# The gated mixer of the second block: 64-column cells instead of 128-column tiles, two step programs instead of one

## The reference

```python
def gated_delta_rule(q, k, v, g, beta):            # mixer A, 4 heads, chunks of 64
    decay = where(causal, exp(gcum_i - gcum_j), 0)
    lmat = where(strict, einsum(kb, kc) * decay, 0)
    uw = triangular_solve(lmat + eye, concat([vb, kb * exp(gcum)], -1))
    attn_intra = einsum(qc, kc) * decay
    def step(state, xs):
        v_new = u_ - w_ @ state
        o = qd @ state + a_ @ v_new
        state = state * exp(gl) + kd.T @ v_new

def mlstm_chunkwise(q, k, v, i_log, f_log):        # mixer B, 4 heads, chunks of 64
    def step(carry, xs):
        pmat = qk_ * exp(d_ - mt)
        num = inter * (q_ @ c_st) + pmat @ v_
        den = inter * (q_ @ n_st) + sum(pmat, -1)
        hout = num / maximum(abs(den), exp(-mt))
        c_st = sc * c_st + kw.T @ v_
        n_st = sc * n_st + sum(kw, -2)

def mixer_ab(hn, ...):
    proj = hn @ w_in                               # 1024 -> 4112
    qkv = silu(causal_conv(proj_a, conv_w)); qa, ka = l2norm(q), l2norm(k)
    oa = rmsnorm(gated_delta_rule(...), norm_a) * silu(z)
    ob = rmsnorm(mlstm_chunkwise(...), norm_b) * sigmoid(o_gate)
    return concat([oa, ob], -1) @ w_out
```

## Time and profile before

| | us |
|---|---|
| median of 3 runs | 3643.74 (3643.6 to 3644.13) |
| the profiled execution | 3643.23 |
| its span (first to last instruction) | 3641.0 |
| TensorE busy / VectorE / ScalarE / GpSimd | 3367.5 / 1598.1 / 1181.9 / 132.3 |
| mean granted TensorE clock | 0.938 |
| projection of the mixer, first L420 to the output projection's first | 1874.4 to 2373.8 |

### The profile page before, as it was taken

The page is one execution under the profiler, slowest core; times in us unless marked ns, Lnnn a source line. Parts: engine busy times, 40 slices in busy tenths (PEclk is TensorE's granted clock), DMA queues, the critical chain, the costliest instruction groups (busy, mean ns, idle before and its releaser), DMA issues. The chain is left out here.

```text
span 3641.0 us, 41271 instructions
## 1 busy us (share of the span) xinstructions
PE 3367.5 (92%) x16842; PEld 2672.2 (73%) x16842; DVE 1598.1 (44%) x2420; ACT 1181.9 (32%) x1910; POOL 132.3 (4%) x148
## 2 busy tenths in 40 slices
PE   7888899999998899999978999989999877899998
PEld 5555577888887566788867787878887655688886
DVE  2144544334354355545553533144334436444344
ACT  2134433223133244433343423133223424432232
POOL 0012200000000021000000210000000000000000
PEclk9899999999998999999977999579999887889999
DMA  6500014432222100223221111013222120122321
GB/s 249 199 1 1 7 56 146 145 122 82 64 70 75 58 1 30 86 93 99 93 68 42 47 35 47 1 64 95 97 93 87 52 73 1 64 70 94 98 94 63
DMA packets 73354, 269.43 MB, mean 74 GB/s; under 512 B 8136, under 2 KB 9032, under 8 KB 71888
## 3 DMA queue, kind: packets, MB, share of 16 engines
q1 hardware_dynamic: 73168, 266.80, 21.8%
HBM read 264.67 MB, written 2.10 MB: 73 GB/s over the span
## 5 line engine op out<-in xcount | busy, mean ns | idle before, releaser
L420 PE MATMUL PS<-room,WHI 128*128 128x512 f32 (+1 forms) x7200 | 2050.1, 382 | 53.5 <-DVE room L704 13.8
L420 PEld LDWEIGHTS PS<-room,WHI 128*128 128x128 f32 x7200 | 1273.1, 192 | 345.8 <-issue 96.4
L420 PE MATMUL PS<-room,WLO 128*128 128x512 f32 (+1 forms) x3600 | 1246.8, 376 | 0.0
L420 PEld LDWEIGHTS PS<-room,WLO 128*128 128x128 f32 x3600 | 641.3, 191 | 127.1
L376 DVE TENSOR_TENSOR WLO<-RING,WHI 128x1024 fp32r<-128x1024 f32 x371 | 453.8, 1223 | 375.5 <-ACT WHI L367 374.6
L367 ACT ACTIVATE WHI<-RING 128x1024 fp32r<-128x1024 f32 x371 | 389.9, 1053 | 544.6 <-PE PS L420 530.7
L826 DVE SCALAR_TENSOR_TENSOR H<-PS,VEC,H 128x511 f32<-128x511 f32 (+1 forms) x132 | 83.1, 657 | 310.1 <-ACT H L804 310.1
L804 ACT ACTIVATE H<-PS,VEC 128x512 f32<-128x512 f32 (+1 forms) x132 | 88.4, 704 | 351.2 <-PE PS L420 351.2
L1257 PE MATMUL PS<-room 96*128 96x256 f32 (+1 forms) x432 | 154.3, 476 | 11.2 <-ACT SQ L1368 7.7
L763 DVE SCALAR_TENSOR_TENSOR X<-PS,MOD,X 128x512 f32<-128x512 f32 x96 | 60.5, 658 | 219.9 <-PE PS L420 219.8
L1463 DVE TENSOR_REDUCE room<-PS 128x1 f32<-128x768 f32 (+1 forms) x120 | 101.9, 849 | 99.1 <-PE PS L1257 98.6
(11 more groups left out here) (344 smaller groups left out, 2988.3 us busy)
## 6 DMA issues: line engine op xcount, KB each, us to landing
RING<-in_stream SPq DMA_DIRECT2D x370, 512.0 KB, 3.4
room<-in_w_ada SPq DMA_DIRECT2D x84, 512.0 KB, 5.6
H<-in_w_ada SPq DMA_DIRECT2D x12, 512.0 KB, 4.5
room<-in_consts SPq DMA_DIRECT2D x4, 1024.0 KB, 9.7
room<-in_wq SPq DMA_DIRECT2D x2, 1728.0 KB, 7.5
X<-in_x_in SPq DMA_DIRECT2D x2, 1536.0 KB, 10.2
room<-in_wple SPq DMA_DIRECT2D x2, 1024.0 KB, 4.8
out_dram<-H SPq DMA_DIRECT2D x8, 256.0 KB, 2.0
```

What stands on the lines that cost most here:

```text
L420: mm = pe.matmul(acc, wt[:, w], xt[:, k * xw + lo:k * xw + lo + q], start=(k == 0 and z == 0), stop=(k == kt - 1 and z == 2))
```

## The change

The chunk matrices of mixer A and B (`LT`, `ATT`, `T`, `TT`, `Y`, `BT`, `DEC`, `DECB`, `ATB`) are no longer 128 wide block diagonals. Chunk n lies as a 64x64 cell on partitions 0 to 63 (n even) or 64 to 127 (n odd), four cells side by side, so that a head's matrix is 256 columns wide and not 512. VectorE, ScalarE and GpSimd work on 256 columns there. On TensorE each matmul of 128x128 becomes two of 64x64, whose rows and output partitions are those of the chunk: even chunks use the first quarter of the array, odd ones the last.

The generators are two for each engine (`pe_chain` and `pe_side`, and so on), both advanced at each tick; a step waits for its tick with `until`. The side program has the query norms, the key by query matrices, the value transposes and A's final spread. `product(i)` and `update(i-1)` now share a tick. Mixer A's first chunk starts the state with a copy and the last makes no state; in B the same, B's state alternates between two buffers, the denominators gather in bank 6 and are taken once at the end. The order of units puts B's values first and A's gate z last.

```diff
-AB_UNITS = ([("gates", 0)] + [("A", 4 + h) for h in range(4)] + [("A", h) for h in range(4)] + [("A", 8 + h) for h in range(4)]
-            + [("A", 12 + h) for h in range(4)] + [("B", h) for h in range(8)] + [("B", 12 + h) for h in range(4)]
-            + [("B", 8 + h) for h in range(4)])
+AB_UNITS = ([("gates", 0)] + [("B", 12 + h) for h in range(4)] + [("A", 4 + h) for h in range(4)] + [("A", h) for h in range(4)]
+            + [("A", 8 + h) for h in range(4)] + [("B", h) for h in range(8)] + [("B", 8 + h) for h in range(4)]
+            + [("A", 12 + h) for h in range(4)])
...
+    cell = lambda name, h, n: c.a(o[name] + h * HALF + (n // 2) * CHUNK, CHUNK, *rows(n))
+    rows = lambda n: (CHUNK * (n % 2), CHUNK * (n % 2) + CHUNK)
+    small_bank = lambda b, n, lo=0: c.bank(b, CHUNK, lo + (n // 2) * CHUNK, *rows(n))
...
-    def idle(n):
-        for _ in range(n):
+    def until(name, tick):
+        while clock[name] < tick:
             yield
...
     def pe_chain(pe):
-        yield from idle(24)
+        yield from until("pe", 42)
...
+        for h in range(4):
+            yield from until("pe", 44 + 8 * h)
+            unit_columns(pe, stat["K"], o["SQK"], h)
...
-            for t in range(4):
-                mm = pe.matmul(c.bank(b, P, t * P), c.a(o["BT"] + (i % 2) * NL + t * P, P), part("T", h, t), start=True, stop=True)
+            for n in range(NCH):
+                mm = pe.matmul(small_bank(b, n), cell("BT", i % 2, n), cell("T", h, n), start=True, stop=True)
             mm.then_inc(*y.up())
...
         for i in range(21):
+            yield from until("pe", 98 + i)
             if i < 20:
                 product(i)
-            yield
             if i:
                 update(i - 1)
-            yield
...
         for n in range(NCH):
+            yield from until("pe", 200 + 3 * n)
+            if n < NCH - 1:
+                for h in range(NH2):
+                    b = ds_bank(n, h // 2)
+                    if h % 2 == 0:
+                        own(pe, (b,), m_state.at(n + 1))
+                    mm = pe.matmul(c.bank(b, VW, (h % 2) * VW), part("KDB", h, t, *r), vt(t, h, VW, *r), start=True, stop=True)
+                mm.then_inc(*m_ds.up())
...
+            for h in range(NH2):
+                pe.matmul(num(h), vt(t, h, P, *r), cell("ATB", h, n), start=(h == 0), stop=(n == 0), skip_group_check=True)
+                mm = pe.matmul(den(h), cell("ATB", h, n), c.ONES[r[0]:r[1], 0:1], start=(t == 0 and h == 0), stop=(n == 0),
+                               skip_group_check=True)
+            if n:
+                yield
+                pe.wait_ge(*m_state.at(n))
+                for h in range(NH2):
+                    pe.matmul(num(h), st2(n, h, 0, P), chunk("QB", h, n), start=False, stop=True, skip_group_check=True)
+                    mm = pe.matmul(den(h), chunk("QB", h, n), st2(n, h, P, 1), start=False, stop=True, skip_group_check=True)
...
+    chains = {"pe": (pe_chain, pe_side), "act": (act_chain, act_side), "dve": (dve_chain, dve_side)}
+    def advance(name, eng):
+        if name not in begun:
+            begun[name] = [f(eng) for f in chains[name]]
+        going = [next(g, "ended") != "ended" for g in begun[name]]
+        clock[name] += 1
+        return any(going)
```

More of the change, by code:

```diff
@@ L1719, in pe_chain @@
+        for h in range(4):
+            yield from until("pe", 71 + h)
+            unit_spread(pe, stat["K"], 1, h, 2 + h)
+        for h in range(4):
+            yield from until("pe", 76 + 4 * h)
+            own(pe, (2,), dec.at(h + 1))
+            for p in range(2):
+                mm = pe.matmul(c.bank(2, HALF, 0, *rows(p)), pick(h, CHUNK), by_half(row4("GCUM"), p), start=True, stop=True)
+            mm.then_inc(*g_bank.up())
             yield
             own(pe, (4,), lt_a.at(h + 1))
-            for t in range(4):
-                mm = pe.matmul(c.bank(4, P, t * P), part("KA", h, t), part("KA", h, t), start=True, stop=True)
@@ L1735, in pe_chain @@
-            own(pe, (7,), v_out.at(h + 1))
-            pe.wait_ge(*silu.at(9 + h))
-            for t in range(4):
-                mm = pe.transpose(c.bank(7, P, t * P), part("VA", h, t), c.ID[:])
-            mm.then_inc(*turn_v.up())
-            yield
+            for n in range(NCH):
+                mm = pe.matmul(small_bank(4, n), chunk("KA", h, n), chunk("KA", h, n), start=True, stop=True)
+            mm.then_inc(*kk.up())
+            own(pe, (3,), lt.at(h + 1))
+            for p in range(2):
+                mm = pe.matmul(c.bank(3, HALF, 0, *rows(p)), pick(h, CHUNK), by_half(row4("BETA"), p), start=True, stop=True)
@@ L1788, in pe_chain @@
+            for n in range(NCH):
+                pe.matmul(c.bank(w_bank(n), CHUNK, (n // 2) * CHUNK), part("KB", h, n // 2, *rows(n)), cell("TT", h, n), start=True, stop=True)
+            for n in range(NCH):
+                mm = pe.matmul(c.bank(4 + h % 2, P, (n // 2) * P, *rows(n)), cell("TT", h, n), part("VB", h, n // 2, *rows(n)),
+                               start=True, stop=True)
             mm.then_inc(*wu.up())
-            yield
         for n in range(NCH):
-            t, r = n // 2, 64 * (n % 2)
@@ L1792, in pe_chain @@
-            lo = t * P + r
-            pe.wait_ge(*(state.at(n) if n else zero.at(1)))
-            own(pe, (2 + n % 2,), vn.at(n + 1))
+            yield from until("pe", 138 + 4 * n)
+            t, r = n // 2, rows(n)
+            new_v = lambda h: c.a(o["VN"] + h * P, P, *r) if n else part("VB", h, 0, *r)
             own(pe, (4 + n % 2,), oa.at(n + 1))
@@ new lines, in pe_chain @@
+            if n < NCH - 1:
+                own(pe, (6 + n % 2,), state.at(n + 1))
+                for h in range(NH2):
+                    mm = pe.matmul(c.bank(6 + n % 2, P, h * P), part("KD", h, t, *r), new_v(h), start=True, stop=True)
+                mm.then_inc(*ds.up())
+            for h in range(NH2):
+                mm = pe.matmul(c.bank(4 + n % 2, CHUNK, h * CHUNK), new_v(h), cell("ATT", h, n),
+                               start=(n == 0 and h == 0), stop=True, skip_group_check=True)
@@ L1833, in pe_chain @@
             own(pe, (4,), m_att.at(h + 1))
-            if h == 0:
-                pe.wait_ge(*b_out.at(8))
-            for t in range(4):
-                mm = pe.matmul(c.bank(4, P, t * P), part("KB2", h, t), part("QB", h, t), start=True, stop=True)
+            pe.wait_ge(*b_out.at(8 + h + 1))
+            for n in range(NCH):
+                mm = pe.matmul(small_bank(4, n), chunk("KB2", h, n), chunk("QB", h, n), start=True, stop=True)
             mm.then_inc(*m_kq.up())
```

671 lines of the change are left out of this document (337 added, 334 removed).

## The result

| | kernel before | changed kernel |
|---|---|---|
| median of the runs shown | 3643.67 us | 3586.16 us (3574.35 to 3591.07) |
| ratio, 95% interval | | 0.9836 (0.982 to 0.9852) |
| profiled execution: span | 3641.0 us | 3589.0 us |
| from the mixer's first triple to the output projection's first | 499.4 us | 444.7 us |
| of that, at half clock | 165 us | 122 us |

The change makes the kernel 57.5 us faster (1.6%), where I forecast 25.5. The time lies inside the mixer, as the forecast had it: before it stand 1874.4 and 1878.3 us, behind it 1267.2 and 1265.9.

The account below looks back on a forecast made before the run. The prediction took TensorE to be the bound throughout, by its instructions and clock, and only at the ends by others. Terms -16 -4 +0 +4 +8 -4.5 -13 = -25.5 took 3643.2 to 3618 us; own range 3600 to 3636, whole range 3572 to 3655.

Parts of the forecast that it names:

- B's loop at full clock: Rival: B's recurrence rises to full clock, -42 us instead of -13, giving 3589 us; chance 0.15.
- Start: Mixer's start: shorter bank wait, no wait for gate rows, gate columns partly at full clock; -16 us (bounds -25 and -6).
- Norm columns: Keys' norm columns come 5 triples behind their unit, and two more waits find other work in front; -4 us.
- Solve: First products, product and update: 960 cell records at 0.045 us, plus shape changes and copy waits, 51 against 51 us: 0.
- Other chunk matrices: Key by key, key by query, products behind the solve, and spread rows: together +4 us (bounds -4 and +16).
- Denser preparation: A head's keys in 4 ticks, not 6: TensorE waits for copies, +4, clock may fall, +4; +8 us (0 to +20).
- A's recurrence: Mixer A: 24 fewer records in first and last chunk, and the wait before B's loop covered by triples; -4.5 us.
- B's recurrence and tail: B's loop to mixer's end: +1 at half clock or -42 at full; clock rises a third of the time, -13 us.
- the rival without it: Quarters of the array don't overlap: 0.058 us a cell record, solve +12, other cells +3, 3633 us; chance 0.18.
- the one with dear cells: Weight load, matmul and quarter change one behind another: 0.08 us a cell record, +45, 3663 us; chance 0.10.
- The clock in the solve: Rival: cells use quarters, so the solve loses its full clock; +38 us, 3656 us; chance 0.07.

Follow-up runs that it names:

- the last run: Changed kernel with B's recurrence grouped by shape, and norm columns, roots, spreads and one value transpose 1 to 5 triples later: 3531.23 us, ratio 0.9688 to the kernel before.
- the second profile: Profile of the changed kernel run again with no edit: 3579.61 us, ratio 0.9823 to the kernel before; mixer 437.6 us, 101 of it at half clock.

## Why the prediction was right and wrong

**The direction and the bound were right.** The time came out of TensorE's own row, inside the mixer, and 3586 lies in the range. It lies outside the forecast's own range of 3600 to 3636. That it lies near the number of a rival, B's loop at full clock (3589), is chance: the loop was granted 0.56 and 0.63 in two profiles.

The terms below are read from the first profile. "Over the triples" means a stretch's time less 0.69 us for each triple in it; for the whole mixer this fell from 317.2 to 262.5 us.

**Start, -16: right.** Start to the end of the gate columns fell from 31.9 to 14.4 us over the triples, -17.5. The wait for the rows went by the later place, as the run with the early columns shows, and the columns took 6.9 (forecast 6.5).

**Norm columns, -4: near.** In front of the key and query columns the waits grew by 4 us (6.2 to 10.4): the squares stand behind other work on ScalarE, and five triples of cover do not reach. The records of these columns and spreads took 2 us less, and A's spreads, 4.1 us behind a wait of 2.9, are now 2.5 without one (the last of them counts with the tail). Together -2. Moved later, these steps were worth most of the 12 to 15 us of the last run.

**Solve, 0: this is one of the two steps that failed.** It came to -15. I priced a cell record at 0.045 us, the middle of two halved rows, 43 us in all. It costs 0.033 with changes of shape in it: 960 records 32.1 us, where 480 took 50.1. The triples there cost 3.4 us more than before over their 0.69 (9.4 us for 39 of them, 6.0 for 46), where I had 5 for changes of shape, and the 3 us of waits for ScalarE's copies did not come. The lower bound, 0.03 from half of L1280's 0.065, was the row to stand by: L1280 is two column halves by turns, as the cells are two quarters by turns, and L1813 is neighbours on one half. That distinction counts for about half of the gain: without the turns a cell costs 0.044, about the price that I had set. In the Trainium skill, TensorEngine Tiling (Array Packing), the section Overview describes the array as independent smaller tiles, four of them at 64x64. I had used the Trainium skill only for its rule against the change. Here 64x64 cells on the two diagonal quarters by turns take 0.032 us against 0.043 on one quarter at a time, a gain of a quarter; by my estimate from that 0.043, two quarters that worked wholly side by side would give 0.022, and no run here shows that.

**Other chunk matrices, +4: too dear.** The 12 groups fell from 11.9 to 7.9 us (I had -0.4), for the same reason. Rows of spreads +1.4 and the two products behind the solve +1.5 came about as forecast. Together -1.

**Denser preparation, +8: the other step that failed.** It came to -7. No step waited for ScalarE's copies. I had argued from ScalarE's busy time in a head's slot; its copies were done before the next head's transposes, which ask for their bank. Nor did half clock add to the time, although the preparation of A itself had more of it (11.8 us against 6.8 from its first decay row to the first products). Ahead of it there were 17.3 us against 27.5, and between A's recurrence and B's 0 against 7. Over their 0.69, and without the waits at norm columns and spreads, the triples between gate columns and solve cost 4.2 us less than before, and those between the recurrences 2.5 less. I had no term for that. No run doubles these copies or moves this work back, so this rests on the profiles, and what lowered the triples' cost stays open; there are also fewer triples in that place (52 against 96).

**A's recurrence, -4.5: right.** 30.8 to 28.0 us, and the wait of 1.7 in front of B's first chunk is gone.

**B's recurrence and tail, -13: near, and the reason right in part.** From the loop's start to the output projection it was 97.3 us over the triples, and is 91.7 in the first profile and 84.5 in the second. Of these 2.5 are three of A's spreads, which stood ahead of the loop before: so -8 and -15. The price at half clock held (0.92 us for a half head), and so did that of the triples. What is missing from my sum for half clock is the matmuls of the chunks that ran at full clock: 48.5 us against 55 for the half heads and 11.4 against 14 for the state sums in the first profile. But only 13% of the loop's time was at full clock there, and 26% in the second profile, where I had a third. The tail's wait shrank as forecast (27.5 us behind the last triple; now 3.4 from the last spread's start):

```profile
2319.62 1.05 PE L1709 MATMUL PS<-ID,room 128*128 128x128 f32 x8
2323.01 0.71 PE L420 MATMUL PS<-room,WHI 128*128 128x512 f32 x2 [2.33 <-DVE room L2272]
```

The terms of the first profile, -17.5 -2 -15 -1 -7 -4.5 -8, give -55; its mixer says -54.7. Of the 29.5 us by which this sum passes the forecast's, 15 are the solve, 15 the preparation and the triples around it, 5 the small matrices and 1.5 the start, less 2 for the norm columns and 5 for B's recurrence. So the forecast fell short mainly by one price, which was a third too high, by one cost that did not come, and by cheaper triples around it, for which it had no term.

**What the rivals had.** Overlap: the rival without it (0.058) and the one with dear cells (0.08) are excluded by 0.032. The clock in the solve stayed at 1.00. What I did not see is the largest reserve of all, in rows that I quoted: the earlier trace rows has four shapes by turns. Their changes were inside my price of a half head, and I never asked what that price would be without them, though B's loop makes 8 to 16 of them in a chunk.

## What to carry to other kernels

Before pricing small matmuls on parts of the array, ask of each row that serves as a price whether its neighbours stand on the same part or by turns on two; take the row of the same pattern, not a mean of both. Then read a loop's timeline for alternating shapes: putting equal shapes side by side is a few lines, and with three triples of full-width work to a chunk it decided here between 0.56 to 0.63 and 0.96 of the clock. Move a step that waits to where its input is ready, and look afterwards at the step that depends on it.

## What the runs showed of the hardware

- A change between matmul shapes costs 0.14 us at full clock (42 more changes, 6.0 us), more than the 0.1 that I took from the trace of before.
- The granted clock of B's loop went with two things at once: shapes by turns with one triple a chunk 0.53 and with three 0.56 to 0.63, equal shapes side by side with one triple 0.60, with three 0.96. Shapes by turns did not bring it down in A's recurrence, where it stood at 1.00 ahead.
- 64x64 cells cost 0.032 us a record when neighbours use two quarters of the array by turns, and 0.043 when they stay on one. A full 128x128 record in the same place costs 0.11 (54.2 us for 480).
- At one change of program the spread of the runs grew from 0.6 us to 17 us in the first set. Two profiles of the same kernel differ by 21 us of half clock in the mixer, and their instructions and waits hardly differ. In later sets the kernel before spread as well (3637 to 3653). What sets this from run to run stays open.
